# One stream of 384 tokens against two: the prompt's pass first in plain 32-bit matmuls, then the samples', with part of the prompt's expert work beside them

## The reference

```python
def trunk_layer(x, cvec, ctx_kv, ...):
    shift1, scale1, gate1, shift2, scale2, gate2 = adaln(cvec, w_ada, b_ada)
    h = rmsnorm(x, g_attn) * (1 + scale1) + shift1
    zf, zq, zk, zv, zp = jnp.split(h @ w_in, IN_SPLITS, axis=-1)
    ...                       # attn: 8 heads x 64, dense or local with cached context
    branch_f = fourier_mix(zf) @ w_fourier
    branch_a = attn @ w_attn
    branch_p = pool_mix(zp, w_pool_grp, pool_scale) @ w_pool
    gf, ga, gp = jnp.split(jax.nn.sigmoid(h @ w_gate + b_gate), N_BRANCHES, axis=-1)
    x = x + gate1 * ((gf * branch_f + ga * branch_a + gp * branch_p) @ w_out)
    h2 = rmsnorm(x, g_ffn) * (1 + scale2) + shift2
    x = x + gate2 * peer_ffn(h2, peer_wq, peer_keys, peer_u, peer_v)
```

## Time and profile before

| | us |
|---|---|
| median of 3 runs | 3137.42 (3128.87 to 3143.71) |
| profiled execution, its own time | 3138.57 |
| span of its trace | 3136.7 |
| TensorE busy | 2641.8 (84%) |
| VectorE busy | 2326.8 (74%) |
| ScalarE, GpSimd busy | 1220.3 (39%), 1345.0 (43%) |

### The profile page before, as it was taken

One profiled execution on the slowest core, in us unless ns is written; L12 is line 12 of the kernel. 1 busy time (PEld: TensorE's weight loads), 2 busy tenths in 40 slices (PEclk: granted clock), 3 DMA queues, 4 the chain that ended last, 5 costly groups with the idle time before them and its releaser, 6 DMA issues.

```text
span 3136.7 us, 42521 instructions
## 1 busy us (share of the span) xinstructions
PE 2641.8 (84%) x14476; PEld 2118.3 (68%) x14476; DVE 2326.8 (74%) x4457; ACT 1220.3 (39%) x2214; POOL 1345.0 (43%) x986
## 2 busy tenths in 40 slices
PE   7899979956899999998969989841679999998995
PEld 1476668235788878877857767631578888887785
DVE  0326545998688888888973554499868988998897
ACT  0213322136344444454432222211645544554553
POOL 0353343347444544343436334423744553443552
PEclk9999989989999999999989999875999999999998
DMA  8832232645999999999963323200589999999995
GB/s 286 268 115 88 93 121 88 229 136 164 349 356 354 351 350 345 354 348 349 349 224 130 101 88 108 105 17 0 161 303 351 361 359 342 368 359 339 349 370 206
DMA packets 241739, 763.15 MB, mean 243 GB/s; under 512 B 32145, under 2 KB 103377, under 8 KB 204369
## 3 DMA queue, kind: packets, MB, share of 16 engines
q1 hardware_dynamic: 156208, 485.56, 43.0%
q0 software_dynamic: 73728, 268.47, 22.9%
q10 hardware_dynamic: 11680, 7.78, 0.9%
HBM read 725.53 MB, written 39.95 MB: 244 GB/s over the span
## 4 chain that ended last, share of the span: by engine, by line
DVE 28%; issue 24%; DMA 24%; POOL 7%; DVEq 7%; PE 5%; ACT 3%; ACTq 1%; POOLq 0%; SPq 0%; PEldq 0%; PEld 0%
DMA raw<-in_experts 21%; POOL wlo L506 7%; DVE wlo L1456 6%; DVE u L1489 6%; DVEq L1491 5%; DVE u L1445 4%; ACT whi L688 3%; PE acc L838 3%; DVE z L1467 3%; DVE u L1322 2%; DVE u L1319 2%; DVE u L1478 1%; PE acc L815 1%; DMA u<-in_u_rows,rowid 1%; DVE z L1326 1%
## 5 line engine op out<-in xcount | busy, mean ns | idle before, releaser
L558 POOL DMA_INDIRECT u<-in_v_rows,rowid x256 | 444.2, 1735 | 786.2 <-DVE z L1467 748.7
L1456 DVE TENSOR_TENSOR wlo<-raw,whi 128x1024 fp32r<-128x1024 f32 x512 | 626.9, 1225 | 173.2 <-ACT whi L688 136.8
L1054 PE MATMUL aux<-lt_hi,whi 128*128 128x256 f32 x2048 | 607.8, 297 | 121.9 <-DVE wlo L1456 121.3
L688 ACT ACTIVATE whi<-raw 128x1024 fp32r<-128x1024 f32 x512 | 537.9, 1052 | 339.8 <-DMA raw<-in_experts 339.4
L1054 PE MATMUL aux<-lt_lo,whi 128*128 128x256 f32 x2048 | 585.1, 286 | 0.0
L1054 PE MATMUL aux<-lt_hi,wlo 128*128 128x256 f32 x2048 | 584.6, 285 | 0.0
L506 POOL TENSOR_TENSOR wlo<-raw,whi 128x1024 fp32r<-128x1024 f32 x144 | 356.4, 2478 | 498.9 <-ACT whi L610 498.9
L1054 PEld LDWEIGHTS aux<-lt_hi,whi 128*128 128x128 f32 x2048 | 396.9, 194 | 200.6 <-DVE wlo L1456 181.0
L1066 PE MATMUL acc<-whi,bt_hi 128*128 128x512 f32 x1024 | 414.5, 405 | 15.0 <-DVE bt_lo L1486 14.8
L1066 PE MATMUL acc<-wlo,bt_hi 128*128 128x512 f32 x1024 | 402.2, 393 | 0.0
L1066 PE MATMUL acc<-whi,bt_lo 128*128 128x512 f32 x1024 | 401.8, 392 | 0.0
(11 more groups left out here) (169 smaller groups left out, 3753.3 us busy)
## 6 DMA issues: line engine op xcount, KB each, us to landing
raw<-in_experts SPq DMA_DIRECT2D x256, 1024.0 KB, 7.3
raw<-in_w_ada SPq DMA_DIRECT2D x96, 512.0 KB, 4.9
gmat<-u SPq DMA_DIRECT2D x32, 1024.0 KB, 5.1
z<-gmat SPq DMA_DIRECT2D x32, 1024.0 KB, 10.4
raw<-in_w_gate SPq DMA_DIRECT2D x24, 1024.0 KB, 5.2
raw<-in_w_in SPq DMA_DIRECT2D x16, 1024.0 KB, 5.5
raw<-in_peer_wq SPq DMA_DIRECT2D x16, 1024.0 KB, 5.1
u<-in_b_gate SPq DMA_DIRECT2D x6, 1536.0 KB, 7.7
```

Of the source, the lines that this page charges most:

```text
L558: pool.indirect_dma_start(VROWS[:, j % GBUF, :], None, a["v_rows"], row).then_inc(vrow_landed[j % GBUF], 16)
L688: act.activation(whi[:, i % SLOTS], raw[:, i % SLOTS], ACT.Copy).then_inc(expert_hi, 1)
L1054: mm = pe.matmul(b[:, 0:TE], w[:, slot, c * P:(c + 1) * P], x[:, c, P:T], start=(c == 0 and i == 0), stop=(c == KC - 1 and i == 2))
L1456: dve.tensor_tensor(wlo[:, i % SLOTS], raw[:, i % SLOTS], whi[:, i % SLOTS].bitcast(F32), ALU.subtract)\
```

## The change

A layer's units are gone through twice. First TensorE does all 72 for the prompt alone (`prompt_unit`): plain 32-bit matmuls, straight from `raw`, with no high and low parts, so ScalarE and GpSimd have no split in it; the prompt's attention, gates and norms lie beside it (`BESIDE_P`). Then SyncE loads the same 72 units again, and `unit` does them for the samples' two blocks (`NB` = 2): 12 matmuls. There are 16 attention steps then, and ScalarE instead of VectorE takes the results of the passes `in0`, `in1`, `q0` and `q1` out.

Beside the samples' passes the prompt's routing is done on VectorE, GpSimd gathers U rows (`gather_u`, five buffers, at the units of `GATHER_AT`), and VectorE takes 56 of the 128 dot products (`EARLY`): 2 after each unit from 26 to 46 and the rest after the columns of the next passes. 72 stay in the expert stage (`DOT_AT` spreads them over the 128 keys). Low parts of the odd units 19 to 47 move from GpSimd to VectorE (`low_part`). V rows get eight buffers. The other parts of the expert stage and the one-hot stage keep their work.

```diff
+NB = 2
+TS = NB * P
+PASSES = (("in0", U_IN, KC), ("in1", U_IN + KC, KC), ("gf", U_GF, KC), ("wf", U_WF, 2), ("gp", U_GP, KC), ("wp", U_WP, 2),
+          ("ga", U_GA, KC), ("wa", U_WA, 4), ("out", U_OUT, KC), ("q0", U_Q, KC), ("q1", U_Q + KC, KC))
+BY_ACT_PASSES = ("in0", "in1", "q0", "q1")
...
+DOTS = {u: 2 for u in range(U_GF + 10, U_OUT)}
+DOTS_MT, DOTS_Q = 4, 8
+EARLY = sum(DOTS.values()) + DOTS_MT + DOTS_Q
+LATE = PICKS - EARLY
+DOT_AT = {(j * KEYS) // LATE: EARLY + j for j in range(LATE)}
...
+UBUF, VBUF = 5, 8
...
+def lo_by_dve(u):
+    return U_GF + 2 <= u < U_OUT and u % 2 == 1
...
+            def gather_u(l, j):
+
+                if l * PICKS + j >= UBUF:
+                    pool.wait_ge(urow_used, l * PICKS + j - UBUF + 1)
+                pool.indirect_dma_start(UROWS[:, j % UBUF, :], None, a["u_rows"],
+                                        bass.IndirectOffsetOnAxis(ap=ROWID[:, j:j + 1], axis=0))\
+                    .then_inc(urow_landed[j % UBUF], 16)
...
+                low_parts(l, U_GF, U_GF + 10)
+                pool.wait_ge(rowid_ready, l + 1)
+                for j in range(UBUF):
+                    gather_u(l, j)
...
+                for u in range(U_GF + 10, UNITS):
+                    if u == U_Q + 4:
+                        root(2 * l + 1)
+                    low_parts(l, u, u + 1)
+                    for j in GATHER_AT.get(u, ()):
+                        gather_u(l, j)
...
+                def prompt_unit(u, x, use, first, last):
+
+                    pe.wait_ge(raw_landed[u // 2 % 2], l * (8 * PAIRS) + 16 * (u // 4 + 1))
+                    s = u % SLOTS
+                    for h in range(2):
+                        if first:
+                            open_acc(use + h)
+                        mm = pe.matmul(accum(use + h)[:], x, raw[:, s, h * HB:(h + 1) * HB], start=first, stop=last)
+                        if last:
+                            mm.then_inc(acc_done, 1)
+                    (pe.drain() if last else mm).then_inc(raw_used, 1)
...
                 def unit(u, lt, chunk, use, first, last, beside=None):
 
-                    pe.wait_ge(lo_ready, l * UNITS + u + 1 + SLOTS)
+                    wait_lo(pe, l, u)
                     s = u % SLOTS
                     for h in range(2):
                         if beside and h:
                             beside()
-                        for t in range(TB):
+                        for t in range(NB):
...
+                dve.tensor_scalar(ROWID[:], ROWF, float(l * KEYS * KEYS), None, ALU.add)
+                dve.drain().then_inc(rowid_ready, 1)
...
+                def low_part(u):
+
+                    dve.wait_ge(hi_ready, l * UNITS + u + 1)
+                    s = u % SLOTS
+                    dve.tensor_tensor(wlo[:, s], raw[:, s], whi[:, s].bitcast(F32), ALU.subtract).then_inc(lo_dve, 1)
...
+                for i in range(U_OUT - U_GF):
+                    u = U_GF + i
+                    if u + 2 < U_OUT and lo_by_dve(u + 2):
+                        low_part(u + 2)
...
+                    if u + 1 < U_OUT:
+                        for _ in range(DOTS.get(u, 0)):
+                            dot(taken)
+                            taken += 1
...
-                    dve.wait_ge(urow_landed[n % GBUF], l * (16 * PICKS // GBUF) + 16 * (n // GBUF + 1))
-                    dve.scalar_tensor_tensor(PROD, UROWS[:, n % GBUF, :], 1.0, H2A, ALU.mult, ALU.mult,
-                                             accum_out=DOT[:, n:n + 1]).then_inc(urow_used, 1)
-                    dve.drain().then_inc(dot_ready, 1)
+                    if n in DOT_AT:
+                        dot(DOT_AT[n])
+                        dve.drain().then_inc(dot_ready, 1)
```

More of the change, by code:

```diff
@@ L130, in build @@
+ACC_USE, ACC_FREE, AUX_USE, AUX_FREE = _bank_tables()
+assert all(AUX_USE["g", l, 0] % 2 == 0 for l in range(DEPTH))
 def build(nc, a, o):
@@ L589, in squares, with modulation @@
+            def squares(n):
+                for t in range(NB):
+                    if n:
+                        act.wait_ge(x_ready, (n - 1) * NB + t + 1)
+                    act.activation(XN[:, t], X[:, 1 + t], ACT.Square, scale=D ** -0.5, accum_out=ms[:, 1 + t:2 + t])
                     act.drain().then_inc(ms_ready, 1)
-            def modulation(n, use, p):
-                if not (isinstance(n, int) and p < 2):
+            def modulation(n, p):
+                if n or p >= 2:
                     act.wait_ge(modr_used, n * 6 + p - 1)
@@ L601, in hi @@
+                for j in range(2):
+                    queries_prompt(j)
+                for j in range(2):
+                    scores_prompt(j)
+                passed("p", "q1", zp(D))
+                act.drain().then_inc(pqp_ready, 1)
                 def hi(u):
@@ L861, in turned_pass @@
                             ready(k)
-                            turn(src, base, k)
+                            turn(kind, src, k)
+                        if between:
+                            between(k)
                         if k >= 3:
@@ new lines, in layer, with residual @@
+                columns("ms", MRAW, lambda k, b: dve.tensor_copy(MRAW[:, k], b[:, 0:TS]))
+                for _ in range(DOTS[U_OUT - 1] + DOTS_MT):
+                    dot(taken)
+                    taken += 1
+                def residual(use, gates, xtmp):
+                    parts = [(h, t) for t in range(NB) for h in range(2)]
+                    for n in range(5):
+                        if n < 4:
+                            h, t = parts[n]
+                            dve.tensor_tensor(xtmp[:, n % 2], accu(use + NB * h + t)[:], gates[:, h * HB:(h + 1) * HB],
+                                              ALU.mult).then_inc(acc_free["v"], 1)
+                        if n:
+                            h, t = parts[n - 1]
+                            at = slice(h * HB, (h + 1) * HB)
+                            dve.tensor_tensor(X[:, 1 + t, at], X[:, 1 + t, at], xtmp[:, (n - 1) % 2], ALU.add)
+                        x = dve.drain()
+                        if n in (2, 4):
+                            x.then_inc(x_ready, 1)
@@ new lines, in layer, with top_keys @@
+                dve.wait_ge(gate1_landed, l * 16 + 16)
+                residual(ACC_USE["s", l, "out"], GATE1, XTMP)
+                dve.sem_inc(out_done, 1)
+                normalise(2 * l + 1)
+                columns("h2s", HRAW, modulate(1))
+                for _ in range(DOTS_Q):
+                    dot(taken)
+                    taken += 1
+                assert taken == EARLY
+                dve.drain().then_inc(dot_ready, EARLY)
+                def top_keys(t, m):
+                    dve.wait_ge(scores_ready, l * (2 * NB) + m * NB + t + 1)
+                    top16([(Z[:, t, k * P:(k + 1) * P], SV[:, t, k, :], SI[:, t, k, :]) for k in range(8 * m, 8 * m + 8)])
+                    dve.drain()
@@ L1359, in layer, with gates @@
+                for t in range(NB):
+                    top_keys(t, 0)
+                def gates(t):
+                    dve.wait_ge(exp_ready, l * NB + t + 1)
+                    shares(SEL[:, t, 2])
+                    dve.drain().then_inc(sel_ready, 1)
+                for t in range(NB):
                     s = t % 2
```

1635 lines of the change are left out of this document (1024 added, 611 removed).

## The result

The changed kernel takes 3221.14 us (median of 4, 3211.02 to 3225.69) against 3138.78 us for the kernel before in the same runs: 1.0262 times as long, 95% interval 1.0226 to 1.0298. The forecast was 3211. The sum came out near, but two of its terms were off by some 30 us a layer each, in opposite directions; most of what follows is about these two. Times of these three are compared with that.

What follows compares the result with a forecast made beforehand. TensorE paces the weight units, VectorE the top-k; TensorE, VectorE and DMA all near their limit in the experts. 3138.57 + 129 + 127 - 21 - 32 - 65 - 65 = 3211 us; range 3100 to 3290.

Steps and rivals of the forecast that it cites:

- The prompt's pass: First pass over 72 units: 164 us paced by the two-pair weight ring, plus small steps; 190 a layer, bounds 150 and 219.
- The samples' passes: Second pass over the units with scores: 12 matmuls a unit, VectorE late or pacing in places; 383 us a layer.
- The stall of 21: TensorE's wait before unit 18, whose copies stand behind the prompt's routing on VectorE: 21 us.
- the two waits behind gathers: Low parts held behind gathers in GpSimd's queue: 7 us in the output projection, 8 in each of two query passes.
- units 25 to 43: Stretch of the samples' passes paced by VectorE with attention steps and dots: 136 us, VectorE over 90% busy as a sign.
- The routing: Prompt's routing done alone on VectorE before unit 18's copies in the samples' passes: 57 us, from 26 on.
- The contention itself: VectorE and GpSimd keeping each other from running in units 25 to 43: 16 us, three quarters of GpSimd's 22.
- The experts: Expert stage: 56 keys lose gather and dot, landing shortens to 6.8; -65 us a layer, bounds -38 and -91.
- Rival A: VectorE doesn't pace the samples' passes: no stall, faster units, no held gathers; 78 a layer shorter, 3055 us; chance 0.18.
- Rival D: Expert stage not relieved, landing stays 7.3, gain only 38 a layer: 3265 us; chance 0.15.
- Rival C: TensorE's waits in the prompt's pass keep its clock at 1.2 GHz: 250 us, 60 a layer more, 3331; chance 0.06.
- Rival B: Prompt's pass paced by TensorE as pairs land during use: 150 us, 40 a layer less, 3131; chance 0.10.

Runs made afterwards that it cites:

- these three: Runs on another chip, where the kernel before took 3160.57 us: changed kernel with low parts on VectorE, changed with four V buffers, kernel before with five U and seven V.
- the run with thin loads: Changed kernel, each load in the prompt's pass bringing only 16 of 1024 columns of its two units, TensorE's work the same: 3177.2 us.
- without dots: Changed kernel with no early dot products, all 128 kept in the expert stage: 3202.2 us.
- the pair of low-part runs: Changed kernel with all low parts on GpSimd, 3235.6 us; and with those of units 18 to 47 on VectorE, 3209.3 us on another chip.
- the same twelve buffers: Kernel before, V gather ahead of U gather: five U and seven V buffers 0.9976 of before; four U and eight V 0.9832.
- four and eight: Kernel before with four U and eight V buffers, V gather ahead of U gather: 3084.93 us (median of 6), 0.9832 of before.

## Why the forecast came out as it did

*The prompt's pass* (190 forecast, 182 and 185 measured with its turns): the sum came out, with parts that cancel. Waiting for weights was booked at 39 (164 less 125) and cost 23 and 22; all else was booked at 150 and is 156 and 159 in the run with thin loads.

*The samples' passes* (383 forecast, 430 and 420 measured) were sized too low, with the right mechanism. The stall of 21 was 20.11, the two waits behind gathers were 7.8 and 10.6, and units 25 to 43 took 135 and 134 where 136 were forecast, with VectorE busy for 88%, a little under the 90% given as a sign. Four parts were too small. The routing took 75 and 71 instead of 57, because the contention of the earlier trace rows comes back at operations beside which GpSimd makes a low part (14.5 and 12 us); the forecast had booked it for the later stretch, not here. Units 18 to 24 took 34 and 33 instead of 30. From the first matmul of the attention projection to the output projection 31 and 30 passed instead of 16: the dots after the last units stand ahead of the merge in VectorE's order, and without dots it is 19 and 20. The rest, from the output projection on, was 128 and 126 instead of 116; where these 10 to 12 come from stays open. (Two slips in the sum itself are small: 26 and 57 make 83 and not 85, and the first unit's terms make 5.05 and not 5.4.)

*The contention itself* was sized well (16 us forecast for units 25 to 43; 16.7 and 16.7 in units 24 to 43, and 72% of GpSimd's time by the pair of low-part runs). Here the Trainium skill (GPSIMD Engine Reference, Specifications), which says that GpSimd's memory interfaces are shared with VectorE, agrees with 4.33 against 2.29 us; that all of GpSimd's time is lost, as the prediction read it, the 16.7 us do not bear out.

*The routing stage* (-21 and -32 forecast) gave 22 and 36.

*The experts* (-65 a layer forecast, 95 and 79 measured) gained more, in layer 0 beyond the 91 that the forecast named as a sign of being wrong. One reading beneath it was short: the window of the earlier trace rows ends at 1596.0, but the last expert matmul at 1611.8, so the stage was 830 and not 815. The step that failed is the one that put all of the gain on dots and gathers leaving: these are worth 54 to 60, close to the 65. The eight V buffers, which the forecast's sum does not hold at all, added 28 to 35.

So a sum 32 to 36 a layer too low on the passes and 14 to 30 too low on the experts' gain ended 10 us from the measured time. That is luck: an error in the passes was made good by a gain that the forecast did not know of. With four V buffers, the kernel that its sum describes, the time was 3291.30, measured once, against 3160.57 for the kernel before, 1.041 times as long, some 130 us where 73 were forecast. Rival A falls: VectorE does pace the passes from unit 25 on, though less of it was at stake than the 43 us that rival A counts, since without dots these 19 units still take 105 and not 93. Rival D falls: landing shortened to 6.5. Rival C falls: the granted clock of the prompt's pass is 0.96 and 0.95. (Its 60 a layer leaves out the 25 of the small steps; it would be 85.) Rival B falls: 182 and 185, not 150.

Of the whole change, the early dots are a net loss of about 20 us, two streams with a second pass over the weights cost the most (181 + 354 us without dots against 446 a layer), and the V buffers' gain does not need the streams: it is had in the kernel before, with 49 us.

## What to carry to other kernels

Work that is moved to where an engine looks half idle should be counted with everything else in that stretch, and with what its neighbour loses beside it; moving a piece off the pacing engine can slow it if the piece runs longer elsewhere and holds it up meanwhile. When a stage gains more than the removed work explains, undo the small edits beside it one by one: here a buffer count that was not in the sum held a third of the gain. And look at which event releases a gather, not only at how many are in flight: the same twelve buffers gave 0 or 1.7%, depending on how they were divided, and so on the instruction that the issuing queue waits for. A total that comes out near its forecast says little until its terms are compared one by one.

## What was not expected of the hardware

Where a V gather is issued at the end of VectorE's row add, its issue on GpSimd took over 3 us in 63 of 236 cases (3.74 in a row above) and 1.14 at the median; with four and eight, where it follows the U gather, in 1 of 256, and 0.94 at the median. The Trainium skill (DMA: Bandwidth & Descriptors, SWDGE vs HWDGE vs iDMA) says that GpSimd writes its descriptors into on-chip memory out of which VectorE locks it in its two-port mode; the long issues fit that, though no run here tells this cause from another. The transfer of 16 of 1024 columns in place of 1 MB saved only 23 us over 36 pairs, as TensorE's own work and the small steps stay.
